# Output projection by token tiles, with the second norm under the next tiles

## The chip, the cores and the metric

One core of a Trainium2 chip runs the whole kernel as one program. The metric is the device time of one execution in microseconds (us). Three executions of the kernel before took 1961.41 us in the median (1959.69 to 1968.96). The engines are TensorE (PE), VectorE (DVE), ScalarE (ACT), GpSimd (POOL) and SyncE (SP, which here only sends DMA requests). A matmul writes PSUM, eight banks of 512 columns; everything else lies in SBUF.

## The reference

One layer of a decoder on 1024 prompt tokens and 64 sample tokens (8 sequences of 8), width 1024. Two groups of heads, dilated attention and retention, are followed by

```
mix = concatenate([att, ret_out(ret, g, gain)])          # tokens x 1024
x   = x + g_a * dot(mix, w_out)                           # output projection, gated residual
z   = rms(x) * (1 + sc_f) + sh_f                          # second norm
x   = x + g_f * dot(square(relu(dot(z, w_ff1))), w_ff2)   # MLP, 4096 wide
y   = rms(x) * (1 + sc) + sh                              # final norm
```

`rms(x)` divides a token's row by the root of its mean square. `g_a`, `sc_f`, `sh_f` and so on come from the conditioning vector: one row for all prompt tokens, one per sequence for the sample. All is float32. The matmuls get float32 accuracy from two rounded parts: every operand is split into a high part and a low part (the operand less its high part), and a product is hi·hi + hi·lo + lo·hi.

## The kernel before, in words

The kernel is a row of stages, each a block of instruction streams, one per engine, that meet at a barrier at the block's end. Within a block the engines wait on semaphores alone, and each engine, and SP's queue of DMA requests, does its work strictly in the order written. The stages are: modulation and first projection, prompt attention, sample heads and cache attention, prompt retention (`stage_prompt_retention`, L1002), output projection (`stage_output`, L1897), MLP (`stage_mlp`, L2026). The order around the change is thus written by hand; there is no planner.

The output projection takes `mix`, held by features (128 features on the partitions, eight such groups `k`, tokens along the row) as `mix_hi` and `mix_lo`, with 64 sample tokens in `mix_s`. A unit of TensorE's work is one tile of 128 tokens and one half (512) of the output columns: 24 matmuls of 512 columns (16 for the sample tile), L2019. The loop runs over the two column halves outside and the nine tiles inside, and uses six PSUM banks in turn. SP loads the first half of `w_out` in four quarters as soon as the block opens (L1925), then the gate rows, the residual input `x` tile by tile, then the second half into the same room. ScalarE makes high parts (L1961), VectorE low parts (L1982). A finished unit is multiplied by the gate by VectorE (L1994), added to `x` by GpSimd (L1953), and squared and summed by ScalarE (L1975). After the second half of a tile SP stores its rows to DRAM (`x1`), since the MLP needs the room of `x` and reads the residual back at its end.

The MLP's block opens with `norm_part` (L320): the root of all nine sums, a scale of each tile by its inverse root (ScalarE L357, VectorE L381), transposes on TensorE to features (L414), scale and shift per feature on VectorE (L396), high parts on ScalarE (L362), low parts shared by VectorE and GpSimd (L349). The weights of the MLP's first group of 256 hidden features are loaded at the block's start, split by ScalarE (L2080) and GpSimd (L2084). Then GpSimd clears the accumulators `y`, `ys`, `hid_s` (L2147 to L2149), and TensorE begins with `first(0)` (L2406), whose second unit waits for the whole of `norm_part`.

Of the kernel before, what the change touches and what calls it, by code (L numbers as in the profile page):

```python
# [24 lines left out]
ds = bass.ds  # L25
# [976 lines left out]
def stage_prompt_retention(nc, io, ps, ident, mix_hi, mix_lo, heads):  # L1002
# [5 lines left out]
    with st.ctx:  # L1008
# [15 lines left out]
        tables, silu_done = st.sem("tables"), st.sem("silu_done")  # L1024
        vg_in = [st.sem(f"vg_in{a}") for a in range(2)]
# [18 lines left out]
        def _(sp):  # L1044
            for a in range(2):
# [143 lines left out]
        def _(pe):  # L1189
# [68 lines left out]
            turn_output(1, 1)  # L1258

# [637 lines left out]
def stage_output(nc, io, ps, mod_p, mix_hi, mix_lo, mix_s, x, xs, ss):  # L1897
# [3 lines left out]
    NCH, OUTS, BANKS = D // CH, TT + 1, 6  # L1901
    QUARTERS = 4
    quarter = lambda q: slice(q * KT // QUARTERS, (q + 1) * KT // QUARTERS)
    with st.ctx:
        raw = st.sb("raw", [P, KT, CH])
        w_hi = [st.sb(f"whi{s}", [P, KT, CH], F32R) for s in range(NCH)]
        w_lo = [st.sb(f"wlo{s}", [P, KT, CH], F32R) for s in range(NCH)]
        gate, gate_s = st.sb("gate", [P, D]), st.sb("gate_s", [NS, D])
        row = [st.sb(f"row{s}", [P, CH]) for s in range(2)]
        sq = st.sb("sq", [P, CH])  # L1910
        raw_in = [st.sem(f"raw_in{q}") for q in range(QUARTERS)]
        x_in = [st.sem(f"x_in{t}") for t in range(TT + 1)]
        g_in, gs_in, w_hi_done, w_lo_done, made, lo_done, sum_done, gated, added, squared, put, zeroed = (st.sem(n) for n in (
            "g_in", "gs_in", "w_hi_done", "w_lo_done", "made", "lo_done", "sum_done", "gated", "added", "squared", "put", "zeroed"))
        columns_in = st.sem("columns_in")
        wv = io["w_out"].rearrange("o (k p) n -> p (o k) n", p=P)
        block = st.block()

        @block.sync
        def _(sp):  # L1920
            def weights(c):
                for q in range(QUARTERS):
                    if c:
                        sp.wait_ge(w_lo_done, q + 1)
                    sp.dma_start(raw[:, quarter(q), :], wv[:, quarter(q), c * CH:(c + 1) * CH]).then_inc(raw_in[q], 16)  # L1925

            weights(0)
            load_rows(sp, io, gate, None, G_A, g_in)
            load_rows(sp, io, None, gate_s, G_A, gs_in)
            load_columns(sp, io, mod_p, (SH_F, SC_F), columns_in)  # L1930
            for t in range(TT):
                sp.dma_start(x[:, t, :], io["x_prompt"][0, t * P:(t + 1) * P, :]).then_inc(x_in[t], 16)
            sp.dma_start(xs[:], io["x_sample"].rearrange("b t d -> (b t) d")).then_inc(x_in[TT], 16)
            weights(1)
            for t in range(TT):
                sp.wait_ge(added, OUTS + t + 1)
                sp.dma_start(io["x1"][t * P:(t + 1) * P, :], x[:, t, :]).then_inc(put, 16)
            sp.wait_ge(added, 2 * OUTS)
            sp.dma_start(io["x1"][S:S + NS, :], xs[:]).then_inc(put, 16)
            sp.wait_ge(put, 16 * (TT + 1))  # L1940
            sp.wait_ge(columns_in, 32)

        @block.gpsimd
        def _(pool):
            pool.memset(ss[:], 0.0).then_inc(zeroed, 1)
            for c in range(NCH):
                for o in range(OUTS):
                    n = c * OUTS + o
                    dst = x[:, o, c * CH:(c + 1) * CH] if o < TT else xs[:, c * CH:(c + 1) * CH]
                    r = row[n % 2][:] if o < TT else row[n % 2][0:NS, :]  # L1950
                    pool.wait_ge(gated, n + 1)
                    pool.wait_ge(x_in[o], 16)
                    pool.tensor_tensor(dst, dst, r, ALU.add).then_inc(added, 1)  # L1953

        @block.scalar
        def _(act):
            act.wait_ge(zeroed, 1)
            for c in range(NCH):
                for q in range(QUARTERS):
                    act.wait_ge(raw_in[q], 16 * c + 16)  # L1960
                    act.copy(w_hi[c][:, quarter(q), :], raw[:, quarter(q), :]).then_inc(w_hi_done, 1)  # L1961
            for c in range(NCH):
                for o in range(OUTS):
                    n = c * OUTS + o
                    if o == TT:
                        act.wait_ge(made, n + 1)
                        act.wait_ge(squared, n)
                        act.copy(sq[0:NS, :], ps[NS:P, n % BANKS, :]).then_inc(lo_done, 1)
                        act.wait_ge(sum_done, c + 1)
                    dst = x[:, o, c * CH:(c + 1) * CH] if o < TT else xs[:, c * CH:(c + 1) * CH]  # L1970
                    rows = slice(0, P if o < TT else NS)
                    act.wait_ge(added, n + 1)
                    if n:
                        act.wait_ge(squared, n)
# [586 lines left out]
```

## Time and profile before

| what | us |
|---|---|
| median of three executions | 1961.41 |
| the profiled execution, its own time | 1961.98 |
| its span in the profile | 1960.1 |
| TensorE busy | 1711.7 (87%) |
| VectorE busy | 829.7 (42%) |
| ScalarE busy | 527.8 (27%) |
| GpSimd busy | 605.3 (31%) |

The times in the rows below count from the start of the span. A timeline row gives start, duration, engine, line of the kernel, operation, `out<-in`, sizes, a count where neighbours of one kind are merged, and in square brackets how long the engine had been idle and what released it. The granted clock (PEclk) is the share of full speed that TensorE was given: 1.00 is 2.4 GHz, 0.50 is 1.2 GHz. Matmuls overlap in the engine, so the distance between two starts is what one costs, not the duration shown.

### The profile page before, as it was taken

To read this page: it belongs to the slowest core of one execution; us is meant where nothing else is said; L and a number is where in the kernel's file an instruction comes from. 1 tells how busy PE (TensorE), PEld (TensorE's weight loads), DVE (VectorE), ACT (ScalarE), POOL (GpSimd) and SP (SyncE) were. 2 spreads that over 40 slices of the span, in tenths; PEclk is the share of its full clock that TensorE was granted. 3 is DMA by queue.
4 is the path that set the end of the run, shared out by engine and by line. 5 is a ranking of instruction groups with operands and counts; after the bars stand their busy time and mean duration, and the time that the engine had idled before them with its cause. 6 is when DMAs were issued, how large, how long until landed. Compare 5 with 4: busy or idle time off the path is not lost. (4 is left out here: it accounts for less than half of the span.)

```text
span 1960.1 us, 22332 instructions
## 1 busy us (share of the span) xinstructions
PE 1711.7 (87%) x8256; PEld 1386.0 (71%) x8256; DVE 829.7 (42%) x1518; ACT 527.8 (27%) x766; POOL 605.3 (31%) x301
## 2 busy tenths in 40 slices
PE   6599999979898678867599589999999999999984
PEld 1488888857777566646478468787878787878863
DVE  4931222036555345564621613333333333333389
ACT  0422222225555155532121321111111111111111
POOL 0333233334100035584112442222222222222355
PEclk9699999979999689886789689999999999999997
DMA  7544443361100767743051221111111111111122
GB/s 267 194 150 138 162 162 119 119 203 39 55 21 18 192 191 222 219 149 101 7 188 76 87 80 44 43 43 43 43 43 43 43 43 43 43 43 43 43 86 91
DMA packets 136428, 192.94 MB, mean 98 GB/s; under 512 B 9643, under 2 KB 84443, under 8 KB 136228
## 3 DMA queue, kind: packets, MB, share of 16 engines
q1 hardware_dynamic: 124246, 169.68, 27.4%
q10 hardware_dynamic: 12128, 22.55, 3.1%
q8 instruction: 32, 0.52, 0.1%
q14 instruction: 22, 0.18, 0.0%
HBM read 163.20 MB, written 29.00 MB: 98 GB/s over the span
## 5 line engine op out<-in xcount | busy, mean ns | idle before, releaser
L2084 POOL TENSOR_TENSOR mlp_w_lo<-mlp_w_raw,mlp_w_hi 128x2048 fp32r<-128x2048 f32 x32 | 148.0, 4626 | 333.0 <-ACT mlp_w_hi L2080 332.8
L2301 DVE TENSOR_TENSOR x<-x,ps 128x512 f32<-128x512 f32 x224 | 153.8, 687 | 142.2 <-PE ps L2477 141.5
L2406 PE MATMUL ps<-mix_hi,mlp_w_hi 128*128 128x512 f32 x512 | 205.9, 402 | 6.8 <-POOL mlp_w_lo L2084 4.8
L2280 DVE TENSOR_TENSOR mlp_h_lo<-mlp_pos,mlp_h_hi 128x512 fp32r<-128x512 f32 x64 | 69.4, 1084 | 325.2 <-ACT mlp_h_hi L2205 323.2
L2406 PE MATMUL ps<-mix_lo,mlp_w_hi 128*128 128x512 f32 x512 | 204.2, 399 | 0.0
L2406 PE MATMUL ps<-mix_hi,mlp_w_lo 128*128 128x512 f32 x512 | 204.1, 399 | 0.0
L2477 PE MATMUL ps<-mlp_w_hi,mlp_h_hi 128*128 128x512 f32 x448 | 175.9, 393 | 5.5 <-PE ps L2412 5.5
L603 POOL TENSOR_TENSOR inp_a_lo<-inp_room,inp_a_hi 128x2048 fp32r<-128x2048 f32 x24 | 110.5, 4604 | 215.6 <-ACT inp_a_hi L649 215.6
L2477 PE MATMUL ps<-mlp_w_hi,mlp_h_lo 128*128 128x512 f32 x448 | 174.4, 389 | 0.0
L2477 PE MATMUL ps<-mlp_w_lo,mlp_h_hi 128*128 128x512 f32 x448 | 174.3, 389 | 0.0
L628 PE MATMUL ps<-inp_whi,z_hi 128*128 128x512 f32 x384 | 151.2, 394 | 10.6 <-DVE inp_wlo L575 7.8
L628 PE MATMUL ps<-inp_wlo,z_hi 128*128 128x512 f32 x384 | 150.4, 392 | 0.0
L628 PE MATMUL ps<-inp_whi,z_lo 128*128 128x512 f32 x384 | 150.1, 391 | 0.0
L1777 POOL TENSOR_TENSOR cache_v_lo<-cache_V,cache_v_hi 128x2048 fp32r<-128x2048 f32 (+1 forms) x19 | 74.1, 3898 | 223.7 <-ACT cache_v_hi L1719 223.7
L2155 POOL TENSOR_TENSOR mlp_pos<-mlp_pos 128x512 f32<-128x512 f32 x64 | 66.7, 1042 | 208.0 <-ACT mlp_pos L2211 208.0
L2406 PEld LDWEIGHTS ps<-mix_hi,mlp_w_hi 128*128 128x128 f32 x512 | 97.5, 190 | 31.8 <-POOL mlp_w_lo L2084 5.1
L2211 ACT ACTIVATE mlp_pos<-ps 128x512 f32<-128x512 f32 x64 | 38.3, 599 | 290.9 <-PE ps L2406 290.9
L2406 PEld LDWEIGHTS ps<-mix_hi,mlp_w_lo 128*128 128x128 f32 x512 | 97.3, 190 | 23.7
L2406 PEld LDWEIGHTS ps<-mix_lo,mlp_w_hi 128*128 128x128 f32 x512 | 97.4, 190 | 23.0
L583 DVE TENSOR_TENSOR x_s<-ps,x_s 9x256 f32<-9x256 f32 x24 | 9.9, 412 | 237.5 <-ACT x_s L666 237.5
L2477 PEld LDWEIGHTS ps<-mlp_w_hi,mlp_h_hi 128*128 128x128 f32 x448 | 84.1, 188 | 25.2 <-issue 8.3
L2477 PEld LDWEIGHTS ps<-mlp_w_hi,mlp_h_lo 128*128 128x128 f32 x448 | 84.1, 188 | 17.7
(361 smaller groups left out, 3456.5 us busy)
## 6 DMA issues: line engine op xcount, KB each, us to landing
mlp_w_raw<-in_w_ff SPq DMA_DIRECT2D x32, 1024.0 KB
inp_room<-in_w_ada SPq DMA_DIRECT2D x16, 1024.0 KB
proj<-inp_row ACTq DMA_DIRECT2D x54, 256.0 KB, 2.4
x<-in_cache_k SPq DMA_DIRECT2D x48, 256.0 KB, 5.2
cache_V<-in_cache_v SPq DMA_DIRECT2D x48, 256.0 KB, 4.7
mod_w<-in_w_ada SPq DMA_DIRECT2D x4, 2048.0 KB, 15.3
x<-in_x_prompt SPq DMA_DIRECT2D x16, 512.0 KB, 11.4
inp_room<-in_w_ada_f SPq DMA_DIRECT2D x8, 1024.0 KB
```

The source lines that it names most:

```text
L583: dve.tensor_tensor(a_row[j % 2], ps[0:NC, 6 + j % 2, 0:AW_CH], a_row[j % 2], ALU.add).then_inc(added, 1)
L603: pool.tensor_tensor(a_lo[:], a_raw[s], a_hi[:].bitcast(F32), ALU.subtract).then_inc(a_ready, 1)
L628: mm = pe.matmul(bank, z[:, k, cols], w[s][:, k, :], start=(k == 0 and a == 0), stop=(k == KT - 1 and a == len(parts) - 1))
L1777: eng.tensor_tensor(v_part(1, q, c), V[:, first:first + count, :], v_part(0, q, c).bitcast(F32), ALU.subtract).then_inc(v_ready, 1)
L2084: pool.tensor_tensor(lo, raw[:], hi.bitcast(F32), ALU.subtract).then_inc(ready, 1)
L2155: pool.tensor_tensor(x, x, x, ALU.mult).then_inc(sq_done, 1)
L2211: act.activation(pos[u % 2][:], ps[:, u, :], ACT.Relu).then_inc(relu_done, 1)
L2280: dve.tensor_tensor(h_lo[s][:, j, cols], pos[u % 2][:], h_hi[s][:, j, cols].bitcast(F32), ALU.subtract).then_inc(h_ready, 1)
L2301: dve.tensor_tensor(dst, dst, ps[:, 5 + o % 3, :], ALU.add).then_inc(added, 1)
L2406: mm = pe.matmul(ps[:, u, :], w[:, k, j * P:(j + 1) * P], z[:, k, rows], start=(k == 0 and a == 0), stop=(k == KT - 1 and a == 2))
L2477: mm = pe.matmul(out, h, w, start=(a == 0), stop=(a == len(parts) - 1))
```

## The change

The output projection runs tile by tile. Both weight halves stay resident; the first half is loaded during the retention stage into a room of its own (`w_room`), which later serves the second half and then the MLP's first weights. The first four tiles do column half 0 in a row and then half 1; the sample tile and the last four do both halves one after the other. Four PSUM banks serve the units, the other four (two pairs) the transposes. VectorE does both parts of the residual, inside the PSUM bank and then into `x`. When a tile's second half is added, ScalarE squares and sums the row and takes the root, VectorE refines the inverse root, ScalarE scales the tile in place once its store has landed, and TensorE transposes it behind the second unit of the next tile. ScalarE and VectorE share its feature columns, then make its high and low parts, which replace `mix` in place. The MLP stage loses `norm_part`; its first weights come with the fourth store, their low half moves from GpSimd to VectorE, and GpSimd's clearing stands first in its stream. GpSimd has no work in the output stage.

```diff
 def stage_prompt_retention(nc, io, ps, ident, mix_hi, mix_lo, heads, w_room):
...
+            for q in range(QUARTERS):
+                load_output_weights(sp, io, w_room, w_in, 0, q)
             for a in range(2):
                 sp.wait_ge(states_done, a + 1)
...
+def load_output_weights(sp, io, room, raw_in, c, q):
+    wv = io["w_out"].rearrange("o (k p) n -> p (o k) n", p=P)
+    sp.dma_start(room[:, quarter(q), :], wv[:, quarter(q), c * CH:(c + 1) * CH]).then_inc(raw_in[q], 16)
...
 def stage_output(...)
-    NCH, OUTS, BANKS = D // CH, TT + 1, 6
+    NCH, BANKS = D // CH, 4
+    ORDER = (0, 1, 2, 3, TT, 4, 5, 6, 7)
+    UNITS = [(t, c) for c in range(NCH) for t in ORDER[:4]] + [(t, c) for t in ORDER[4:] for c in range(NCH)]
...
+        pair = lambda m: banks(ps, 4 + 2 * (m % 2), 2)
+        # SP
+            load_rows(sp, io, gate, None, G_A, g_in)
+            for t in ORDER[:4]:
+                tile(t)
+            for q in range(QUARTERS):
+                sp.wait_ge(w_lo_done, q + 1)
+                load_output_weights(sp, io, raw, raw_in, 1, q)
+            load_columns(sp, io, mod_p, (SH_F, SC_F), columns_in)
+            load_rows(sp, io, None, gate_s, G_A, gs_in)
+            load_rows(sp, io, None, scs, SC_F, scs_in)
+            for t in ORDER[4:]:
+                tile(t)
+            for m, t in enumerate(ORDER):
+                sp.wait_ge(added, AT[t, 1] + 1)
+                # store of the tile's rows to x1, put[t]; behind the sample's also:
+                    load_rows(sp, io, None, shs, SH_F, shs_in)
+                if m == 3:
+                    # the MLP's first weights into w1_raw and w2_raw
...
+        # PE
+            def unit(n):
+                if n >= BANKS:
+                    pe.wait_ge(added, n - BANKS + 1)
...
+            def turn(m):
+                t = ORDER[m]
+                pe.wait_ge(xn_done, m + 1)
+                if m >= 2:
+                    pe.wait_ge(lo_done, m - 1)
+                for k in range(KT):
+                    # transpose of 128 columns of x[:, t] into pair(m)
+            for n, (t, c) in enumerate(UNITS):
+                unit(n)
+                m = ORDER.index(t)
+                if c and m:
+                    turn(m - 1)
+            turn(LAST)
+        # ACT, per tile m, after the eight split(c, q)
+                square_and_root(m)      # waits for added; Square with sum, Sqrt
+                if m:
+                    features(m - 1)     # waits for turned; 4 x Identity(scale, bias) 128x128, then copy to mix_hi
+                scale(m)                # waits for r_ready and put[t]; act.mul on x[:, t, :]
+        # DVE, after split(0, 0..3)
+            for n in range(4):
+                residual(n)
+                split(1, n)
...
+            for m, t in enumerate(ORDER):
+                for c in range(NCH):
+                    if c or m >= 4:
+                        residual(AT[t, c])   # bank = bank * gate; x += bank
+                if m:
+                    features(m - 1)          # 4 x tensor_scalar 128x128 from PSUM
+                inverse_root(m)              # five one-column steps
+                if t == TT:
+                    scale_sample(m)          # waits for put, scs_in, shs_in
+                if m:
+                    low_part(m - 1)          # to mix_lo
+            features(LAST)
+            low_part(LAST)
...
 def stage_mlp(...)
-        z_ready, z_half, _, x_read = norm_part(...)
...
         def _(pool):
-            wait_all(pool, x_read)
             pool.memset(y[:], 0.0).then_inc(zeroed, 1)
             pool.memset(ys[:], 0.0).then_inc(zeroed, 1)
             pool.memset(hid_s[:], 0.0).then_inc(zeroed, 1)
...
-            wait_all(act, z_ready)
+            split_hi(act, w1_hi, w1_raw, w1_in, w1_free, w1_hi_done, 0)
...
         def _(dve):
+            split_lo(dve, w1_lo[:], w1_raw, w1_hi[:], w1_hi_done, w1_ready, 0)
...
-            first(0, 0, opening=True)
+            first(0, 0)
```

Lines that begin with `+` and hold a `#` sum up code in words.

## Rows read from the trace of the kernel before

**Rows 1.** Summary by stretches; columns: stretch, us, each engine's busy time, PEclk, DMA, GB/s.

```profile
1018.00:1082.00 64.00, 64.00 (x283) 52.71 (x281) 9.66 (x14) 11.43 (x31) 17.91 (x14) 1.00 0.15 62
```

**Rows 2.** Timeline where the output projection starts; columns: start, us, engine, line, operation.

```profile
977.90 2.50 SPq L1925 DMA_DIRECT2D outp_raw<-in_w_out  x4
...
982.45 1.04 ACT L1961 CAST outp_whi<-outp_raw 128x1024 fp32r<-128x1024 f32 x1 [6.51 <-DMA outp_raw<-in_w_out]
...
983.52 1.22 DVE L1982 TENSOR_TENSOR outp_wlo<-outp_raw,outp_whi 128x1024 fp32r<-128x1024 f32 x1 [6.33 <-ACT outp_whi L1961]
...
984.80 0.79 PE L2019 MATMUL ps<-outp_whi,mix_hi 128*128 128x512 f32 x1 [9.91 <-DVE outp_wlo L1982]
...
990.50 0.39 PE L2019 MATMUL ps<-outp_wlo,mix_hi 128*128 128x512 f32 x1
```

**Rows 3.** Timeline from the last output matmul to the MLP's first.

```profile
1081.65 0.39 PE L2019 MATMUL ps<-outp_wlo,mix_s 128*128 128x512 f32 x1
...
1085.55 0.50 SPq L1939 DMA_DIRECT2D x<-x_s  x1
...
1089.64 0.17 DVE L376 TENSOR_SCALAR mod_p<-mod_p 128x8 f32<-128x8 f32 x1 [5.46 <-PEq L177]
...
1096.02 1.90 ACT L2080 CAST mlp_w_hi<-mlp_w_raw 128x2048 fp32r<-128x2048 f32 x1
...
1118.20 0.77 PE L2406 MATMUL ps<-mix_hi,mlp_w_hi 128*128 128x512 f32 x1 [1.40 <-DVE shift_row L396]
```

**Rows 4.** Groups by line, 975 to 1125; after the bar: busy us, mean ns, idle before.

```profile
L1994 DVE TENSOR_TENSOR outp_row<-ps,outp_gate 128x512 f32<-128x512 f32 x16 | 11.0, 690 | 49.7 <-PE ps L2019 47.7 <-POOL x L1953 2.0
...
L1982 DVE TENSOR_TENSOR outp_wlo<-outp_raw,outp_whi 128x1024 fp32r<-128x1024 f32 x8 | 9.8, 1225 | 26.5 <-ACT outp_whi L1961 26.2
...
L357 ACT ACTIVATE x<-x,mlp_norm_r 128x1024 f32<-128x1024 f32 x4 | 4.3, 1138 | 1.2 <-DVEq L379 1.2
...
L381 DVE TENSOR_SCALAR x<-x,mlp_norm_r 128x1024 f32<-128x1024 f32 x4 | 2.7, 750 | 0.1
```

**Rows 5.** Groups by line in the MLP's tail, 1880 to 1961.

```profile
L2245 ACT ACTIVATE mlp_w_raw<-x 128x1024 f32<-128x1024 f32 x8 | 8.5, 1057 | 38.7 <-DVE x L2361 38.7
...
L2250 ACT ACTIVATE mlp_tail_q<-last_ss,mlp_eps 128x1 f32<-128x1 f32 x9 | 2.7, 295 | 0.3
...
L2316 DVE TENSOR_SCALAR mlp_tail_v<-last_ss 128x1 f32<-128x1 f32 x9 | 1.3, 145 | 0.3 <-ACT mlp_tail_q L2250 0.3
```

**Rows 6.** Eight scalings of 128 columns (timeline); ScalarE's nearest of that size (group).

```profile
917.90 2.64 DVE L953 TENSOR_SCALAR ret_on<-ps,ret_mv 128x128 f32<-128x128 f32 x8
...
L827 ACT ACTIVATE att_prob<-att_prob,att_neg 128x128 f32<-128x128 f32 x8 | 3.2, 402 | 10.8 <-DVE att_neg L878 10.8
```

**Rows 7.** Timeline of TensorE in the cache stage: transposes between matmuls, and after a pause.

```profile
681.75 1.03 PE L1576 MATMUL ps<-ident,x 128*128 128x128 f32 x8
682.54 0.48 PE L1589 MATMUL ps<-mix_hi,cache_q_hi 128*128 128x512 f32 x1
...
687.95 1.97 PE L1576 MATMUL ps<-ident,x 128*128 128x128 f32 x16 [2.41 <-DMA x<-in_cache_k]
```

**Rows 8.** DMA issues, 970 to 1125: count, KB each, median us to landing.

```profile
x<-in_x_prompt SPq DMA_DIRECT2D x8, 512.0 KB, 7.7
x<-x SPq DMA_DIRECT2D x8, 512.0 KB, 2.6
...
x<-x_s SPq DMA_DIRECT2D x1, 256.0 KB, 2.9
```

**Rows 9.** Timeline of VectorE beside GpSimd, in prompt attention and in the second norm.

```profile
433.76 2.53 DVE L885 TENSOR_SCALAR att_prob<-att_prob,att_inv 128x256 f32<-128x256 f32 x1
...
434.33 1.81 POOL L1317 MEMSET q_blocks<- 128x2048 f32 x1
...
1097.99 4.51 POOL L2084 TENSOR_TENSOR mlp_w_lo<-mlp_w_raw,mlp_w_hi 128x2048 fp32r<-128x2048 f32 x1 [12.47 <-ACT mlp_w_hi L2080]
1098.47 4.58 DVE L349 TENSOR_TENSOR mix_lo<-shift_row,mix_hi 128x512 fp32r<-128x512 f32 x1 [1.72 <-ACT mix_hi L362]
```

More of the change, by code:

```diff
@@ L1944, in _, with tile @@
[L1944 to L1953, printed above, removed]
+            def tile(t):
+                if t < TT:
+                    sp.dma_start(x[:, t, :], io["x_prompt"][0, t * P:(t + 1) * P, :]).then_inc(x_in[t], 16)
+                else:
+                    sp.dma_start(xs[:], io["x_sample"].rearrange("b t d -> (b t) d")).then_inc(x_in[TT], 16)
@@ L1955, in _, with split, sample_low @@
         @block.scalar
         def _(act):
-            act.wait_ge(zeroed, 1)
+            def split(c, q):
+                act.wait_ge(raw_in[q], 16 * c + 16)
+                act.copy(w_hi[c][:, quarter(q), :], raw[:, quarter(q), :]).then_inc(w_hi_done, 1)
+            def sample_low(c):
+                act.wait_ge(made, AT[TT, c] + 1)
+                if c:
+                    act.wait_ge(summed, c)
+                act.copy(sq[0:NS, 0:CH], ps[NS:P, AT[TT, c] % BANKS, :]).then_inc(lo_copied, 1)
@@ new lines, in square_and_root @@
+            def square_and_root(m):
+                t = ORDER[m]
+                rows, src = (slice(0, P), x[:, t, :]) if t < TT else (slice(0, NS), xs[:])
+                act.wait_ge(added, AT[t, 1] + 1)
+                act.wait_ge(zeroed, 2)
+                if m:
+                    act.wait_ge(squared, m)
+                act.activation(sq[rows, :], src, ACT.Square, accum_out=ss[rows, t:t + 1]).then_inc(squared, 1)
+                act.wait_ge(squared, m + 1)
+                act.activation(q_root[:, t:t + 1], ss[:, t:t + 1], ACT.Sqrt, scale=1.0 / D, bias=eps[:]).then_inc(rooted, 1)
@@ new lines, in features @@
+            def features(m):
+                t = ORDER[m]
+                act.wait_ge(turned, m + 1)
+                if t == TT:
+                    act.copy(mix_s[:, :, 0:NS], by_feature(pair(m)[:, 0:KT * NS])).then_inc(hi_done, 1)
+                    return
+                if m:
+                    act.wait_ge(lo_done, m)
+                for k in range(KT // 2):
+                    cols = slice(k * P, (k + 1) * P)
+                    ins = act.activation(zf[:, cols], pair(m)[:, cols], ACT.Identity, scale=mod_p[:, J_SC, k:k + 1],
+                                         bias=mod_p[:, J_SH, k:k + 1])
+                ins.then_inc(aff_act, 1)
+                act.wait_ge(aff_act, m + 1 - (m > ORDER.index(TT)))
+                act.wait_ge(aff_dve, m + 1 - (m > ORDER.index(TT)))
+                act.copy(mix_hi[:, :, t * P:(t + 1) * P], by_feature(zf[:])).then_inc(hi_done, 1)
@@ L1962, in _ @@
[L1962 to L1974, printed above, removed]
-                    act.activation(sq[rows, :], dst, ACT.Square, accum_out=ss[rows, c, o:o + 1]).then_inc(squared, 1)
+                    split(c, q)
```

266 lines of the change are left out of this document (159 added, 107 removed).

## The prediction

> **What bounds the kernel now.** The summary by stretches comes first. While the output projection streams its units TensorE is the bound: it has no idle time and the granted clock is 1.00 (2.4 GHz), and 283 matmuls start in 64.00 us, one every 0.226 us [rows 1]. Nothing done beside these matmuls can shorten them; time can only be won where TensorE stands before and behind them. The timeline gives both places. At the front the block opens at 977.90 with the request for the weights, ScalarE gets the first quarter at 982.45, VectorE makes the low half, and TensorE starts at 984.80; it runs its first matmuls at half the rate, the 1.2 GHz level (25 were due in the 5.70 us to 990.50 at 0.226, about 13 were run) [rows 2]. At the back the last matmul starts at 1081.65, the second norm and the split into features run as a stage of their own, and the MLP's first matmul starts at 1118.20, again after idle time [rows 3]. With 0.23 for its own slot the last unit is over at 1081.88, so 36.3 us lie between. The groups by line then give the price of each instruction that is moved.
>
> **The start.** The first half of the weights is loaded in the retention block, whose SP queue holds only two state stores behind it; its four requests took SP 2.50 us before [rows 2], there nobody waits for them. So at 977.9 ScalarE can split at once: 1.04, then VectorE 1.22, then 0.06 to TensorE [rows 2]: first matmul at 980.2, 4.6 us earlier. If the load came late, these 4.6 would be lost and no more. TensorE's 416 matmuls (16 units of 24, two of 16) and their cold first 5 us are as before. The second half must be split before unit 4 (tile 0, columns from 512 on). Its loads now wait only for four low halves and stand before the sample rows in SP's queue; its last low half stands in VectorE's queue behind the residual of unit 3 and ends at about 1007.4, and unit 4 wants it at 1008.6. Slack 1.2 us, cost nothing; each us beyond is paid once.
>
> **Work beside the units.** Two residual instructions go to VectorE, 0.69 each [rows 4], 1.4 a unit, in place of one on VectorE and one on GpSimd. Multiplying inside a PSUM bank is not in the trace; I take the price of PSUM to SBUF, between 0.5 and 0.9. A bank is free 1.65 us after its unit, and with four banks it is wanted three units (16 us) later: nothing. Per tile come Square 1.06 and Sqrt 0.30 on ScalarE, five one-column steps of about 0.15 each, 1.0 with their hand-overs, on VectorE [rows 5], a scale of 1.14, a high part of 1.04 on ScalarE and a low part of 1.22 on VectorE [rows 2, 4], and four feature columns of 128 on each engine: VectorE ran eight of that shape in 2.64, so 1.35 for four; on ScalarE 0.40 is the nearest single one, 1.55 for four [rows 6]. Each engine has 5 to 6.5 us of work a tile against 6.3 (first tiles) or 11.8 (later) of TensorE, so it hides as throughput. GpSimd is left idle.
>
> **What TensorE gains in work: the turns.** Nine turns of eight transposes now stand in its own queue, seven of them ahead of the last unit. In the cache stage eight transposes between matmuls pushed the next one from 681.75 to 682.54 [rows 7]: 0.79, with a hand-over 0.9 each, 7 x 0.9 = 6.3. Before, all of them ran in the gap.
>
> **The wait each turn adds.** A turn waits until its tile is scaled; behind it on TensorE stands the next unit, and behind that everything. From the end of a unit's slot: 0.2 until its last matmul is through (0.39 long, a slot of 0.23) and 1.4 of residual, 1.45 of square and root, then on ScalarE the features of the tile before (1.55 and 1.04) and the scale 1.14: 6.8. The inverse root on VectorE is done beside those features. ScalarE's scale also waits for the store of the tile, 2.6 us after issue [rows 8], which lands before the features are through; behind the scale wait the next tile's square and features. TensorE arrives after 6.3 (24 matmuls, 5.44, and a turn of 0.9): 0.5 us of stall for the second and the third tile. The first tile has no features ahead, so its store decides: 1.65 + 2.6 + 1.14 and a hand-over, 5.5 against 5.44, 0.1. From the fourth on two units lie between, and nothing is late but the sample tile: VectorE waits for shift rows that SP sends as eight requests behind the sample's store, with the low part of tile 3 and the residuals of tile 4 queued behind; I get 0.2, with 0 and 3 as ends. In all 1.3. The weights of the MLP's first group are requested behind the fourth store and nobody stands behind them soon. The last unit ends at 1081.9 - 4.6 + 6.3 + 1.3 = 1084.9.
>
> **The tail.** From there: residual 1.65; square and root to 3.15; the features of tile 6 to 4.7 and their high part to 5.75 on ScalarE; scale to 6.9; last turn at the half clock, twice 0.79 plus the hand-over, to 8.8; features to 10.4; high part 11.5; low part 12.75. The end of the block costs about 1.3 (the sample's store issued at 1085.55, landed 2.9 later, next stage at 1089.64 [rows 3, 8]): 14.0. Then the MLP's own start: ScalarE's copy of the first weights 1.90 [rows 3], VectorE's low half of 2048 columns (1.225 for 1024 and 0.69 for 512 give 2.3 [rows 4]), hand-over 0.1: 18.3. First matmul at 1103.2 instead of 1118.20.
>
> **What may hold that low half.** GpSimd now clears the accumulators as its first act in the MLP block, 8192 columns at the rate of a clearing before (1.81 for 2048 [rows 9]), about 7 us, and VectorE's low half is wanted 2 us into it. Both engines stand in each other's way twice [rows 9]: a scaling with one SBUF operand took 2.53 and ended with GpSimd's clearing, and a subtraction of two SBUF operands took 4.58 and ended with a GpSimd subtraction. No row has the pair needed here, a two-operand subtraction beside a clearing. Ends: 0 and 6.4 us (all clearings). The scaling that was held runs at twice the rate of a subtraction (0.75 against 1.22 for 1024 columns [rows 4]), so it needs two streams out as well as in; the clearing takes a stream out only, and the subtraction needs a second stream in only. I take 0, as the operands do not meet, without being sure. The Trainium skill, page "SBUF — State Buffer", section "Who interferes with whom", says that a VectorE instruction with two SBUF inputs collides with a GpSimd instruction that reads SBUF and not with one that only writes it, but that whichever comes second at the shared ports stands still for the whole of the other's instruction. By that the cost here would be 0. Both held rows agree with it; no run here shows the pair in question.
>
> **Sum.** 1118.2 - 1103.2 = 15.0 us earlier; the rest of the MLP is unchanged, also its wait for the second group's weights, which follows its own start. The profiled execution took 1961.98 (span 1960.1), so 1947.0; the median of the runs is 0.6 lower, 1961.41: 1946.4.
>
> **The rivals.** (1) As summed, 1943 to 1950: chance 0.58. (2) The clearing holds VectorE: start at 7.0 or 8.3 instead of 2.0, so 5.0 to 6.4 given back, 1951 to 1953; for it the 2.53 row, against it that its operation is of another kind. 0.24. (3) The chain of a tile is longer by some us than the unit that covers it: each us costs three in the first tiles and one in the tail. At 1.5 us, 6: 1952. For it, the tie of 6.8 with 6.3; against it, that every piece has a row. 0.11. (4) Slower: the stores of the tiles land late. Place: ScalarE's scale. A 512 KB transfer landed after 2.6 where little else moved and 7.7 among other loads [rows 8]. At 7.7 the scale is late by about 5.0, 3.6 and 3.6 in the first tiles, 2 at the sample and 3.6 in the tail: 17.8 against a gain of 15.0, so 1964; and pauses of 4 to 5 us may take the clock to the 1.2 GHz level, as the 9.91 us did ahead of 984.80, another 2.7 each (25 slots less 13 run, at 0.226) for up to three, 1972. It decides from landings of about 7 us on. Against it: all loads of the block are issued before the first store, which comes some 25 us later. 0.05. (5) The turns and their waits take the clock down: eight times 2.7 is 22, so 1968. Eight transposes between matmuls that took 0.1 each, and 16 that took 0.12 each after a pause of 2.41, are against it [rows 7]. 0.02.
>
> **The numbers.** 0.5% is 9.8 us, about what a measurement here can tell from none. Faster by more: nearly all of (1), half of (2) and (3): 0.55 + 0.12 + 0.04 = 0.71. Slower by more (above 1971.2): the worse parts of (4) and (5), 0.04. The rest, 0.25, within. Range: (1), (2) and most of (3), 1942.5 to 1955.
>
> **What would show it.** First unit at about 980 if the early load works. Seven turns of 0.9 us between units, and pauses of at most 1 us ahead of the first three: if they are 3 us or more, (3) or (4). The last unit's end near 1085, the MLP's first matmul 18 us later; 23 with VectorE's 2048-column subtraction lasting 7 us means (2). A granted clock of 0.5 between units means (5). The prediction is wrong if the stretch between first unit and first MLP matmul is not 123 us (133.4 before) or if the start is not earlier.

## The result and the profile after

The changed kernel takes 1947.77 us in the median of four executions (1942.73 to 1950.54); the kernel before, in four executions now, takes 1965.18 (1959.69 to 1970.17). The ratio is 0.9903, with an interval from 0.9875 to 0.993. 1946.4 was forecast. The profiled execution took 1950.54, its span is 1948.7.

Totals of single executions are a poor measure here: the stages ahead of the output projection, which the change leaves as they were but for four load requests in the retention stage, end between 977.9 and 994.2 us in the profiles of this case (the last section shows one reason, worth 6 to 8 us of it; no run here explains the rest). So most readings below are of one stretch, from the opening of the output block (SP's first request in it) to the MLP's first matmul. It was 140.3 us (977.90 to 1118.20, [rows 2, 3]); it is 124.7 us now (983.23 to 1107.91). That is 15.6 less, and 15.0 was forecast. From the MLP's first matmul to the end of the span it was 841.9 and is 840.8; in the five profiles that have the changed kernel's MLP as it is it lies between 840.8 and 842.1, so this 1.1 is not shown to be a gain. The 15.6 us are 0.8% of the time, which lies inside the interval of the ratio.

The front, as a timeline of the kernel after (start, duration, engine, line, operation, idle time before and its releaser):

```profile
983.23 0.35 SPq L298 DMA_DIRECT2D gate_row<-mod  x1
983.25 3.88 ACT L2024 CAST outp_whi<-w_room 128x1024 fp32r<-128x1024 f32 x4 [1.98 <-PEq L1008]
...
984.33 4.63 DVE L2088 TENSOR_TENSOR outp_wlo<-w_room,outp_whi 128x1024 fp32r<-128x1024 f32 x4 [0.91 <-ACT outp_whi L2024]
985.61 0.79 PE L1997 MATMUL ps<-outp_whi,mix_hi 128*128 128x512 f32 x1 [5.38 <-DVE outp_wlo L2088]
...
989.09 0.39 PE L1997 MATMUL ps<-outp_whi,mix_lo 128*128 128x512 f32 x1
```

ScalarE now splits as soon as the block opens, and TensorE begins 2.4 us behind the opening; it was 6.9 [rows 2]. The slow matmuls are fewer as well: eight start in the 3.48 us to 989.09, where before 13 started in 5.70 [rows 2].

The first turns, same view; the row behind the first turn is the next unit's first matmul:

```profile
1015.75 0.69 DVE L2104 TENSOR_TENSOR x<-x,ps 128x512 f32<-128x512 f32 x1
1016.60 1.06 ACT L2039 ACTIVATE outp_sq<-x 128x1024 f32<-128x1024 f32 x1 [16.91 <-DVE x L2104]
1019.43 1.15 ACT L2065 ACTIVATE x<-x,outp_r 128x1024 f32<-128x1024 f32 x1 [1.34 <-DMA x<-x]
1020.00 0.40 PE L1997 MATMUL ps<-outp_whi,mix_lo 128*128 128x512 f32 x1
1020.63 1.10 PE L2008 MATMUL ps<-ident,x 128*128 128x128 f32 x8 [0.23 <-ACT x L2065]
1021.49 0.48 PE L1997 MATMUL ps<-outp_whi,mix_hi 128*128 128x512 f32 x1
...
1027.08 1.04 PE L2008 MATMUL ps<-ident,x 128*128 128x128 f32 x8
...
1033.80 1.09 PE L2008 MATMUL ps<-ident,x 128*128 128x128 f32 x8 [0.17 <-ACT x L2065]
```

The first tile's scale waits for its store (the releaser is the DMA of `x`), and TensorE loses 0.4 us there (0.63 between the last matmul of the unit and the turn, where 0.23 is a slot). The second turn comes without a wait, the third loses 0.3. From then on the turns stand between the units with nothing but their own time, 0.79 for a prompt tile and 0.64 for the sample tile, and 0.10 of wait at the latter.

The summary by stretches, columns as in [rows 1]:

```profile
1012.00:1089.00 77.00, 76.60 (x363) 62.73 (x362) 44.66 (x104) 35.53 (x64) 0.00 (x0) 1.00 0.24 84
1089.54:1107.91 18.37, 3.02 (x17) 2.37 (x15) 9.63 (x18) 9.37 (x15) 4.37 (x1) 0.64 0.24 71
```

Between the units TensorE stays busy at a granted clock of 1.00, as in [rows 1], while VectorE and ScalarE now have 45 and 36 us of work beside it in 77. From the last unit's end (1089.54) to the MLP there are 18.4 us, where 36.3 were.

The tail as a timeline:

```profile
1095.06 1.14 ACT L2065 ACTIVATE x<-x,outp_r 128x1024 f32<-128x1024 f32 x1
...
1096.25 1.97 PE L2008 MATMUL ps<-ident,x 128*128 128x128 f32 x8 [5.67 <-ACT x L2065]
...
1103.55 6.92 POOL L2281 MEMSET x<- 128x8192 f32 x1 [147.00 <-POOLq L177]
1103.63 1.90 ACT L2233 CAST mlp_w_hi<-w_room 128x2048 fp32r<-128x2048 f32 x1 [2.79 <-SPq L2249]
...
1105.57 2.29 DVE L2237 TENSOR_TENSOR mlp_w_lo<-w_room,mlp_w_hi 128x2048 fp32r<-128x2048 f32 x1 [3.47 <-ACT mlp_w_hi L2233]
1107.91 0.80 PE L2538 MATMUL ps<-mix_hi,mlp_w_hi 128*128 128x512 f32 x1 [9.69 <-DVE mlp_w_lo L2237]
```

It is one chain in which nothing overlaps: scale, a turn at the half clock, features, high and low part, the block's end, the weights' high and low part. GpSimd's clearing runs from 1103.55 to 1110.47, and VectorE's low half of 2048 columns, right inside it, takes 2.29: what two undisturbed rows had given as 2.3.

Groups by line of the kernel after, 983 to 1108 (as [rows 4]), and a row of its DMA issues, 960 to 1115 (as [rows 8]):

```profile
L2101 DVE TENSOR_TENSOR ps<-ps,gate_row 128x512 f32<-128x512 f32 x16 | 11.1, 696 | 29.3 <-PE ps L1997 29.3
L2104 DVE TENSOR_TENSOR x<-x,ps 128x512 f32<-128x512 f32 x16 | 11.0, 687 | 0.5
```

```profile
x<-x SPq DMA_DIRECT2D x8, 512.0 KB, 2.6
```

Multiplying inside a PSUM bank costs 0.696 a unit, as from PSUM to SBUF [rows 4]. The stores land after 2.6 us, as before [rows 8].

### The profile page after: what moved, and what is told of

It is laid out like the page before. It is cut to its first block and busy times, and to the rows that moved or that the text cites. A ratio compares the mean times of both kernels' runs of the same rounds, so it can differ in the third digit from the quotient of the medians.

```text
span 1948.7 us, 22386 instructions
## 1 busy us (share of the span) xinstructions
PE 1705.4 (88%) x8256; PEld 1379.8 (71%) x8256; DVE 846.9 (43%) x1589; ACT 540.9 (28%) x784; POOL 567.6 (29%) x273
## 5 line engine op out<-in xcount | busy, mean ns | idle before, releaser
L2237 POOL TENSOR_TENSOR mlp_w_lo<-w_room,mlp_w_hi 128x2048 fp32r<-128x2048 f32 x31 | 143.5, 4631 | 320.5 <-ACT mlp_w_hi L2233 320.4
L2538 PE MATMUL ps<-mix_hi,mlp_w_hi 128*128 128x512 f32 x512 | 205.5, 401 | 15.2 <-DVE mlp_w_lo L2237 9.7
L2436 DVE TENSOR_TENSOR x<-x,ps 128x512 f32<-128x512 f32 x224 | 153.9, 687 | 142.3 <-PE ps L2609 141.5
L2538 PE MATMUL ps<-mix_lo,mlp_w_hi 128*128 128x512 f32 x512 | 203.7, 398 | 0.0
L2538 PE MATMUL ps<-mix_hi,mlp_w_lo 128*128 128x512 f32 x512 | 203.6, 398 | 0.0
L2609 PE MATMUL ps<-mlp_w_hi,mlp_h_hi 128*128 128x512 f32 x448 | 175.9, 393 | 5.6 <-PE ps L2544 4.7
L2609 PE MATMUL ps<-mlp_w_hi,mlp_h_lo 128*128 128x512 f32 x448 | 174.5, 389 | 0.0
L2609 PE MATMUL ps<-mlp_w_lo,mlp_h_hi 128*128 128x512 f32 x448 | 174.3, 389 | 0.0
L2538 PEld LDWEIGHTS ps<-mix_hi,mlp_w_hi 128*128 128x128 f32 x512 | 97.2, 190 | 40.2 <-DVE mlp_w_lo L2237 10.1
L2538 PEld LDWEIGHTS ps<-mix_hi,mlp_w_lo 128*128 128x128 f32 x512 | 97.0, 189 | 23.7
L2538 PEld LDWEIGHTS ps<-mix_lo,mlp_w_hi 128*128 128x128 f32 x512 | 97.2, 190 | 22.9
L2609 PEld LDWEIGHTS ps<-mlp_w_hi,mlp_h_hi 128*128 128x128 f32 x448 | 84.1, 188 | 25.4 <-issue 8.4
L2609 PEld LDWEIGHTS ps<-mlp_w_hi,mlp_h_lo 128*128 128x128 f32 x448 | 84.1, 188 | 17.7
```

Source lines behind the costliest of these rows:

```text
L2237: pool.tensor_tensor(lo, raw, hi.bitcast(F32), ALU.subtract).then_inc(ready, 1)
L2436: dve.tensor_tensor(dst, dst, ps[:, 5 + o % 3, :], ALU.add).then_inc(added, 1)
L2538: mm = pe.matmul(ps[:, u, :], w[:, k, j * P:(j + 1) * P], z[:, k, rows], start=(k == 0 and a == 0), stop=(k == KT - 1 and a == 2))
L2609: mm = pe.matmul(out, h, w, start=(a == 0), stop=(a == len(parts) - 1))
```

## The experiments

The theory is the forecast's: the gain is the wait of TensorE ahead of the first unit and behind the last, less the turns that now stand in its queue. In each kernel one term of that is changed by itself. The first four kernels and the last were executed once each; they are read by the stretch, which came out at 124.68 and 124.75 us in the two profiles of the changed kernel. In the code, `...` stands for lines left out, a comment behind a line or in place of one sums up code, and `<...>` an expression.

### The first half's loads at the block's opening

```diff
-            for q in range(QUARTERS):
-                load_output_weights(sp, io, w_room, w_in, 0, q)      # retention block
+            for q in range(QUARTERS):
+                load_output_weights(sp, io, raw, raw_in, 0, q)       # first in the output block
             load_rows(sp, io, gate, None, G_A, g_in)
```

> The changed kernel with one part undone: the first half of the output weights is requested when the output block opens, not in the retention block. Measured from the block's opening (SP's first request) to the MLP's first matmul: 124.7 us in the changed kernel (983.23 to 1107.91), 140.3 in the kernel before (977.90 to 1118.20). Theory (the early load is worth what TensorE no longer waits at the front, and nothing later takes it back): first output matmul 6.9 us after the opening instead of 2.4, all behind it as before, 124.7 + 4.5 = 129.2, to be seen within 128.2 to 130.2. Rival (the stage is set by the chain of the tiles and by its loads, not by when it begins): the stretch grows by less than 1.5 us, 124.7 to 126.2, and the pauses of TensorE ahead of the first turns (0.47 and 0.40 now) vanish or the second half's split stops being in time. Second rival (it costs more, since four quarters, gate rows and four tiles of x now come through one queue at once and the first residuals wait for their rows): over 131.

The stretch is 130.8 us (984.25 to 1115.04), 6.1 more and not 4.5. The first matmul comes 6.98 behind the opening, as expected of the front.

The front, where the block opens at 984.25:

```profile
991.23 0.80 PE L1997 MATMUL ps<-outp_whi,mix_hi 128*128 128x512 f32 x1 [10.00 <-DVE outp_wlo L2088]
...
996.88 0.40 PE L1997 MATMUL ps<-outp_wlo,mix_hi 128*128 128x512 f32 x1
```

The rest is in the pace of the matmuls behind it: 13 start in the 5.65 us to 996.88, as before the change, instead of eight in 3.48, which is five times 0.2 or 1.0 us; and up to the first turn, 30 us later, they come 0.2333 apart instead of 0.2290, 0.6 us on 130. The chain of the tiles took back 0.1 at the turns. So undoing the early load cost 4.6 of waiting, and 1.0 of slow matmuls that the forecast had left out. The 0.6 is not shown to belong to it: the kernel with loads beside the stores keeps the early load and has the same 0.2333 up to its first turn (below).

### A clearing that reads

```diff
-            pool.memset(y[:], 0.0).then_inc(zeroed, 1)
+            pool.tensor_tensor(y[:], y[:], y[:], ALU.subtract).then_inc(zeroed, 1)
```

> The changed kernel, but GpSimd clears the first accumulator by subtracting it from itself (8192 columns, two reads and a write) instead of writing zeros. In the changed kernel the clearing took 6.92 us from 1103.55 and VectorE's low half of 2048 columns, 1105.57 to 1107.86, took 2.29 beside it. Theory (what GpSimd reads decides: a clearing that only writes leaves VectorE's subtraction alone, one that reads holds it): GpSimd's subtraction takes about 18 us (4.51 for 2048 columns, four times), VectorE's low half begins 2 us into it and ends only with it, so the MLP's first matmul comes about 16 to 18 us later, 140 to 143 us after the output block's opening (124.7 now). Rival A (GpSimd and VectorE do not meet here at all, and the two slow rows of before had another cause): low half 2.3, first matmul at 124.7. Rival B (they share and both are slowed to half, none is held to the end): low half about 4.6, first matmul at 127.

Timeline of this kernel where the MLP opens:

```profile
1098.62 13.84 POOL L2281 TENSOR_TENSOR x<-x 128x8192 f32<-128x8192 f32 x1 [147.07 <-POOLq L177]
...
1100.62 13.99 DVE L2237 TENSOR_TENSOR mlp_w_lo<-w_room,mlp_w_hi 128x2048 fp32r<-128x2048 f32 x1 [3.47 <-ACT mlp_w_hi L2233]
...
1114.66 0.79 PE L2538 MATMUL ps<-mix_hi,mlp_w_hi 128*128 128x512 f32 x1 [21.39 <-DVE mlp_w_lo L2237]
```

VectorE's low half, the same instruction on the same data, is 13.99 long instead of 2.29. It ends at 1114.61, 2.15 behind GpSimd's end at 1112.46: about its own time, counted from there. It was held whole; neither rival gives that (2.3 and 4.6). The stretch is 136.4, 11.7 more. That the number misses 140 to 143 is the price of GpSimd's instruction: 13.84, not 18, since it reads one tile for both operands (in the kernel before, GpSimd's instructions on 512 columns take 1.04 with one tile twice, L2155, and 1.29 with two tiles, L1953). The pair that no row of before showed is thus shown on both sides: a two-operand subtraction on VectorE beside a GpSimd instruction that only writes takes 2.29, as long as with GpSimd idle (1071.87 in the kernel with the MLP's first weights split under the units), and beside one that reads it waits to its end.

The Trainium skill, page "SBUF — State Buffer", section "Who interferes with whom", says that a VectorE instruction with two SBUF inputs contends with a GpSimd instruction that reads SBUF and not with one that only writes it; here it agrees, with 13.99 and 2.29.

### Every turn twice

```diff
-                for k in range(KT):
+                for k in [*range(KT)] * (2 if m < LAST else 1):
```

> The changed kernel with each turn but the last done twice over (8 more transposes of the same tile into the same place). Theory (a turn between units stands in TensorE's queue and costs its own time, 0.79 for a prompt tile and 0.64 for the sample tile, and nothing hides it): 7 x 0.79 + 0.64 = 6.2, less what the pauses ahead of the first turns give back (0.87 in all), so the stretch from the output block's opening to the MLP's first matmul grows from 124.7 to between 130.0 and 131.1, with the granted clock at 1.00 between the units. Rival (TensorE has room there, since another chain sets the pace): under 126. Rival (more transposes between the matmuls take the clock down): over 135, with a granted clock under 1.00 there.

```profile
1019.80 1.97 PE L2008 MATMUL ps<-ident,x 128*128 128x128 f32 x16 [0.26 <-ACT x L2065]
1021.52 0.48 PE L1997 MATMUL ps<-outp_whi,mix_hi 128*128 128x512 f32 x1
...
1100.75 1.97 PE L2008 MATMUL ps<-ident,x 128*128 128x128 f32 x8 [4.79 <-ACT x L2065]
```

```profile
1018.00:1094.00 76.00, 75.75 (x391) 63.27 (x390) 42.96 (x96) 34.10 (x61) 0.00 (x0) 1.00 0.22 77
```

The stretch is 130.0 (982.45 to 1112.41), 5.3 more: a turn costs its own time, also the second time (16 transposes move the next matmul by 1.72, eight by 0.86), and the clock stays at 1.00. The lower end of what was expected is met, not its middle, because eight turns were doubled there and only seven lie ahead of the last unit: the eighth falls into TensorE's own wait, which shrank from 5.67 to 4.79.

### Loads beside the stores

```diff
-            for t in ORDER[4:]:
-                tile(t)
             for m, t in enumerate(ORDER):
                 # store of the tile
+                if m == 0:
+                    for late in ORDER[4:]:
+                        tile(late)
```

> The changed kernel with the loads of the sample rows and of tiles 4 to 7 of the residual input requested right behind the first store instead of ahead of it, so that the stores of the second and third tile go out among 2.25 MB of loads. This is the case that the slower forecast was built on. Theory (the scale of a tile waits for its store; landings of 2.6 us just fit, and a landing late by n us costs n once per tile that has one unit for cover): the second store, requested about 4 us ahead of its tile's scale, lands after 6 to 9 us instead of 2.6, TensorE pauses 2 to 5 us ahead of the second turn and 0 to 4 ahead of the third, and the stretch from the output block's opening to the MLP's first matmul grows from 124.7 to between 127 and 133. Rival (stores are not held up by loads behind and beside them, or the chain has slack for it): no pause over 1 us, 124.5 to 125.5.

```profile
988.78 0.40 PE L1998 MATMUL ps<-outp_whi,mix_lo 128*128 128x512 f32 x1
...
1016.63 0.35 SPq L1967 DMA_DIRECT2D x<-x  x1
...
1020.27 0.39 PE L1998 MATMUL ps<-outp_whi,mix_lo 128*128 128x512 f32 x1
...
1020.72 1.15 ACT L2066 ACTIVATE x<-x,outp_r 128x1024 f32<-128x1024 f32 x1 [2.47 <-DMA x<-x]
1021.92 1.09 PE L2009 MATMUL ps<-ident,x 128*128 128x128 f32 x8 [1.26 <-ACT x L2066]
1022.15 15.94 SPq L1967 DMA_DIRECT2D x<-x  x3
...
1028.48 1.15 ACT L2066 ACTIVATE x<-x,outp_r 128x1024 f32<-128x1024 f32 x1 [2.37 <-DMA x<-x]
1029.69 1.09 PE L2009 MATMUL ps<-ident,x 128*128 128x128 f32 x8 [1.16 <-ACT x L2066]
```

The stretch is 127.3 (982.94 to 1110.20), 2.6 more. The second store, requested at 1022.15, lets its scale begin only at 1028.48, 6.3 later, and TensorE pauses 1.2 us ahead of each of the first two turns instead of 0.2 and none. Around the first three turns that is 2.0 us more than in the kernel after, where the third turn waited as well. The other 0.6 is pace: from 988.78 to 1020.27, the last matmul ahead of the first turn, the starts are 0.2333 apart (135 distances), and behind the turn 0.229 as in the kernel after. The mechanism of the slower forecast is real and costs each pause once, but 2.25 MB of loads right behind the first store make TensorE wait 1.2 us ahead of two turns, where rival (4) had five tiles late by 2 to 5 us, 17.8 in all. The pauses were expected at 2 to 5.

### The kernel after, again

> The changed kernel once more, on the chip of the next three, as their yardstick. Expected: 1943 to 1951 us; from the output block's opening to the MLP's first matmul 124.7, to the first matmul of the MLP's second group 158.4, as in the first profile (983.23, 1107.91, 1141.60), each within 0.5, while the block's opening itself, which unchanged stages set, lies anywhere between 978 and 985.

1948.22 us in the median of six (1945.08 to 1960.89), ratio to the kernel before 0.9902 (0.9874 to 0.9931), with 1968.36 for that in the median of twelve. The stretch is 124.75 us and the time from the opening to the MLP's second group of 256 hidden features 158.46, as in the first profile, though the block opens at 993.51, 10.3 us later; 978 to 985 was expected for that, and missed.

### The MLP's first weights split under the units

```diff
                 scale(m)
+                if m == 6:
+                    act.wait_ge(w1_in, 16)
+                    act.copy(w1_first[0][:], w1_raw).then_inc(w1_hi_made, 1)
...
                     low_part(m - 1)
+                if m == 6:
+                    dve.wait_ge(w1_hi_made, 1)
+                    dve.tensor_tensor(w1_first[1][:], w1_raw, w1_first[0][:].bitcast(F32), ALU.subtract).then_inc(w1_lo_made, 1)
```

> The changed kernel, but the first 256 hidden features' weights of the MLP are split inside the output block, by ScalarE and VectorE under the units of the tile before last; their low part lies where the second weights of that group were, and these are loaded once the first four units of the MLP are through. Theory (the last chain ahead of the MLP is serial, so its two weight instructions, 1.90 and 2.29 with 0.1 between, come off the time whole, and both engines have room for them under the units, which take 11.9 us a tile against 7): the MLP's first matmul comes 14.2 us after the last output unit's end instead of 18.4; from the output block's opening to the MLP's second group 158.4 - 4.2 = 154.2. Rival (the two instructions delay the tile's own chain by the same amount): the last turn comes later, 157 to 158.4. Rival (the second weights, now loaded about 25 us later, are late): second group as in the theory, but TensorE waits ahead of the first output units of the MLP for weights, over 2 us.

```profile
1069.94 1.89 ACT L2084 CAST w_first_hi<-w_room 128x2048 fp32r<-128x2048 f32 x1
1071.87 2.29 DVE L2181 TENSOR_TENSOR w_first_lo<-w_room,w_first_hi 128x2048 fp32r<-128x2048 f32 x1 [1.63 <-ACT w_first_hi L2084]
...
1101.32 0.79 PE L2549 MATMUL ps<-mix_hi,w_first_hi 128*128 128x512 f32 x1 [5.51 <-SPq L2259]
```

The MLP's first matmul comes 14.2 us behind the last unit's end (1087.12) and waits for the block's end alone, no longer for weights. From the opening (980.83) to the second group (1134.76) it is 153.9, 4.5 less. Neither rival shows: the last output unit ends 106.3 behind the opening as before, and ahead of the MLP's first output units TensorE waits 0.39, as in the kernel after. 1945.03 us in the median of five; the ratio to the kernel before, 0.9901 (0.9869 to 0.9933), cannot tell 4.5 us from the kernel after.

### Two of the MLP's units under the tail

```diff
...
+            early_unit(0)        # 24 matmuls: first 512 tokens, hidden features 0 to 127
             turn(LAST)
+            early_unit(2)        # the same tokens, hidden features 128 to 255
```

> As the kernel with the early split, and besides TensorE computes two of the MLP's first four units (those of the first 512 tokens, whose features are long there) in the output block, one ahead of the last turn and one behind it. Theory (what is left of the tail is TensorE waiting for one tile's chain, and any work that doesn't need this tile fills it): the two units, 10.9 us, come out of the MLP; the second of them ends about 0.5 us after the last low part, which moves the block's end by no more; the last turn runs at the full clock, 1.0 sooner. From the output block's opening to the MLP's second group 154.2 - 10.5 = 143.7 (142.5 to 145). Rival (the last turn, behind a unit of 5.45 us and the seventh turn, comes late and the chain behind it too): up to 1 us more, 144.7. Rival (the MLP's first group is bound by its weights' loads and the chain of its hidden features, not by TensorE): over 148, with longer waits ahead of the second group than the 4.84 of now.

```profile
1001.39 0.41 PE L1998 MATMUL ps<-outp_whi,mix_lo 128*128 128x512 f32 x1
...
1107.87 1.09 PE L2009 MATMUL ps<-ident,x 128*128 128x128 f32 x8 [0.21 <-ACT x L2078]
...
1116.20 0.47 PE L2561 MATMUL ps<-mix_hi,w_first_hi 128*128 128x512 f32 x1 [1.77 <-SPq L2271]
```

The last turn waits 0.21 instead of 5.67 and takes half the time. From the opening (994.15) to the second group (1138.43) it is 144.3; 143.7 was expected. The 0.6 more lie at the front: eleven slow matmuls start in the 4.86 us from 996.53 to 1001.39 (granted clock 0.50), behind the same pause of 5.38 us that eight follow elsewhere, so the last output unit ends 107.0 behind the opening and not 106.3. 1934.69 us in the median of five, ratio 0.9829 (0.9794 to 0.9864).

### The second group's weights early as well

```diff
+            sp.dma_start(w1_raw, <columns 256 to 511 of w_ff1>).then_inc(w1_in, 16)   # end of the output block
...
+            act.copy(w1_hi[:], w1_raw).then_inc(w1_hi_done, 2)                         # MLP opening, ScalarE
+            split_lo(dve, w1_lo[:], w1_raw, w1_hi[:], w1_hi_done, w1_ready, 1)         # MLP opening, VectorE
```

> As the kernel before it, and besides the weights of the MLP's second group are requested at the end of the output block and split at the MLP's opening by ScalarE and VectorE, beside GpSimd's clearing, instead of by ScalarE and GpSimd behind the first group's hidden features. Theory (in the changed kernel TensorE waits 4.84 us ahead of the second group for GpSimd's low part and then runs 12 matmuls at the half clock; nothing else is late there): the wait goes, and 2 us of clock with it, so from the output block's opening to the second group 143.7 - 4.8 = 138.9 (138 to 140), and the total some 21 us under the changed kernel, 1925 to 1930. Rival (the wait is taken over by the sample's hidden features or the second weights): the wait ahead of the second group or of the first output units of the MLP stays at 3 us or more, total over 1931. Rival (VectorE's low half beside the clearing is held after all): it takes 5 us or more instead of 2.3.

```profile
1104.84 6.94 POOL L2307 MEMSET x<- 128x8192 f32 x1 [147.77 <-POOLq L177]
...
1106.85 2.29 DVE L2260 TENSOR_TENSOR mlp_w_lo<-w_room,mlp_w_hi 128x2048 fp32r<-128x2048 f32 x1 [5.04 <-ACT mlp_w_hi L2395]
...
1121.85 0.44 PE L2586 MATMUL ps<-ident,mlp_hid_s 128*128 128x128 f32 x2 [3.60 <-DVE mlp_hid_s L2455]
```

```profile
1105.18:1122.05 16.87, 13.28 (x67) 11.15 (x67) 6.92 (x9) 6.65 (x10) 11.83 (x7) 1.00 0.15 52
```

The kernel after, where its second group starts:

```profile
1141.60 0.79 PE L2538 MATMUL ps<-mix_hi,mlp_w_hi 128*128 128x512 f32 x1 [4.84 <-POOL mlp_w_lo L2237]
```

That wait of 4.84 us for the weights is gone. A wait of 3.60 for the sample's hidden features, just ahead of the second group, remains; it was 2.08 in the kernel after and 3.89 in the kernel before this one, so the wait of 3 us or more that the first rival named is there, but not its total over 1931. The clock stays at 1.00 through the MLP's first units, and VectorE's low half is again 2.29 beside the clearing. From the opening (983.80) to the second group (1122.05) it is 138.3; 138.9 was expected. 1927.94 us in the median of six (1924.69 to 1930.99), ratio 0.9796 (0.977 to 0.9822): faster than both kernels, and 40 us under the kernel before where the change alone is 20 under it.

### Work for TensorE while it waits at the front

```diff
+            for n in range(6):
+                pe.matmul(ps[:, 4, :], mix_hi[:, 0, 0:P], mix_hi[:, 0, 0:CH], start=True, stop=True)
             for n, (t, c) in enumerate(UNITS):
```

> As the kernel with the second group early, and TensorE begins the output block with six matmuls of 128x512 into a PSUM bank that nothing reads, in the 2.4 us in which it waits for the first low half of the weights. It weighs the step of the prediction that let the slow matmuls at the front be as before: with the pause ahead of the first unit at 10 us 13 matmuls came 0.43 apart, at 5.38 us 8 did. Theory (the slow stretch counts from when TensorE begins to work again, whatever the work is, so matmuls in the wait use it up): the first unit has 2 to 4 slow matmuls instead of 8, and from the block's opening to the end of the last output unit it takes 0.8 to 1.2 us less than the 106.3 of now. Rival (the length of the slow stretch comes from how long the pause was and begins with the unit): 8 slow ones as before, 106.3. Second rival (the idle matmuls, six at 0.43 or 2.6 us, end after the weights are there): first unit 0.3 later and the gain smaller by as much, 105.6 to 105.9.

```profile
983.26 2.90 PE L2017 MATMUL ps<-mix_hi 128*128 128x512 f32 x6 [3.06 <-PEq L1008]
985.95 0.63 PE L2000 MATMUL ps<-outp_whi,mix_hi 128*128 128x512 f32 x1
...
988.93 0.40 PE L2000 MATMUL ps<-outp_wlo,mix_hi 128*128 128x512 f32 x1
```

Nothing won: seven slow matmuls of the first unit instead of eight, the first one 0.4 later, and 106.4 us to the last unit's end where it was 106.3. My theory fell, which wanted two to four slow matmuls there. The first rival has the time right (106.3), but not the place where the slow stretch begins: the six idle matmuls are slow as well. The full rate comes 5.72 us behind the opening (988.93), where it came 5.86 behind it without the idle matmuls (989.09 in the kernel after). Slow matmuls were 13 behind a pause of 9.91, 13 behind 10.00, 6 + 7 behind 3.06, and behind 5.38 eight in seven profiles and eleven in one; these runs don't tell what sets the number.

## Why the prediction was right, step by step

**The start.** 4.6 forecast, 4.5 measured (2.38 behind the opening, not 6.90), and undoing it alone gave it back. The sentence that TensorE's cold first 5 us are as before was wrong: they are 1.0 us shorter in this profile (and 0.3 in the one with eleven slow matmuls).

**The second half.** No wait of TensorE for it. The low half ended 28.8 us behind the opening (1010.79 and 1.22), within 0.7 of the forecast.

**Work beside the units.** Hidden, as said: the prices were right (0.696 and 0.687 a residual instruction), and the only waits that reach TensorE are those of the first and third turn and 0.10 at the sample tile.

**Turns and waits.** 6.3 and 1.3 forecast. Summing the distances between starts around the seven turns, less 0.229 a slot, gives 7.0 together: about 6.1 of turns (with the slot behind each 0.09 longer) and 0.84 of waits (0.40, none, 0.34, and 0.10 at the sample tile). The first was put at 0.1: its scale began 2.97 us behind the store's request, where 2.6 was counted. The waits at the second and third tile were counted as 0.5 each. But a wait ahead of the first turn moves TensorE, and not the second tile's chain, which has begun with its own unit's end: the second then has none. The terms were thus mis-sized one by one, and their sum came out 0.6 too large.

**One term that was in no step.** In the output projection the matmuls come 0.2291 us apart in the profiles of the changed kernel, and 0.2267 before: 1.0 us over 416. It cancels the 1.0 of the shorter cold stretch, so that the last unit ends 106.3 behind the opening where 107.0 was forecast. That it comes from the change is not shown, and no run was made to find its cause. Other paces stand beside it at a granted clock of 1.00: 0.2333 up to the first turn in two of the kernels above, and in the MLP, before and after alike, 0.233 in the first product (L2406, L2538) and 0.227 in the second (L2477, L2609).

**The tail.** 18.3 forecast, 18.4 measured, with the turn at the half clock. Its 4.2 us for the weights and its rest were then taken off piece by piece in three runs, and each came out within 0.7 of the number expected.

**The clearing.** Taken as 0, and 0. The reason given (streams out against streams in) is the one that the clearing that reads confirms: it would have cost 11.7 there. The other half of the reason, that the held scaling of [rows 9] needs two streams out, no run has tested. So rival (2), held at 0.24, was ruled out for a writing clearing, and only for that.

**Rivals (3) to (5).** The tile's chain was as long as forecast (last matmul of its unit at 1020.00, scale done at 1026.90: 6.9 less a slot is 6.7, against 6.8), so (3) had no ground. (4) needs landings that the order of the loads prevents; forced, they cost 2.0 of waits. (5) is excluded by the clock of 1.00, also with twice the transposes.

**The total.** 15.6 in the stretch and 1.1 in the MLP make 16.7 in the two profiles; they show only 11.4 between them, since the earlier stages were 5.3 us later in the second. From the first unit to the MLP's first matmul, the stretch that the prediction named as its test, it is 122.3, with 123 forecast and 133.4 before. That the total of 1946.4 came within 1.4 of the result is luck: the base of the forecast, 1961.41, was a low median of three, 3.8 under the 1965.18 of four (and 7.0 under the 1968.36 of twelve), and the gain of the medians is 17.4, 2.4 over the 15.0 of the forecast. The gain of the stretch, 15.6, is what bears the prediction out.

## What to carry to other kernels

Where the bounding engine has no idle time, look only at what it waits for in front and behind, and price what is moved as the instructions it adds to that engine's queue. Once the norm lies under the units, what is left of the tail is one tile's serial chain: fill it with work of the next stage that needs other tiles, and take the weights' preparation out of it; in the last kernel but one that brought 20 us more, as much as the change itself. Beside a two-operand instruction of VectorE let GpSimd write, not read.

## What was not expected of the hardware

The retention stage, in which the change moves no work but four load requests, has two lengths. From its gain request to the opening of the output block it took 95.2 to 95.5 us in eight of the eleven profiles, and 101.4 to 103.0 in three (the second run of the kernel after among them), with and without the early weight load. So the early load shows no cost there. The request itself came between 881.8 and 892.7, which no run here explains. The same two stretches of that stage, each counted from its gain request (887.75 and 890.52), in the first profile of the kernel after:

```profile
945.00:960.00 15.00, 13.81 (x97) 11.23 (x95) 7.68 (x26) 3.63 (x3) 9.03 (x2) 1.00 0.02 5
957.75:977.75 20.00, 8.09 (x39) 5.93 (x38) 15.35 (x63) 1.45 (x3) 0.00 (x0) 0.68 0.00 0
```

and in the second:

```profile
947.77:962.77 15.00, 13.81 (x81) 11.23 (x79) 5.84 (x11) 3.90 (x3) 9.02 (x2) 0.73 0.02 5
960.52:980.52 20.00, 17.55 (x53) 12.43 (x52) 8.50 (x32) 1.23 (x2) 0.00 (x0) 0.50 0.00 1
```

In the one TensorE is granted 1.00 (2.4 GHz) for a burst of 97 matmuls, in the other 0.73, and the next stretch stays at 0.50 (1.2 GHz); the burst follows the same 1.19 us pause in both. The two lengths lie 6 to 8 us apart, so between single executions they can hide half of a gain of 15.6.
